# Zero products at the start, the second tile's output product by column halves, and identity products among the last rows

## The reference, cut to what matters

```python
h = rms_norm(x, norm2_g)                  # 256 x 1024
aff = softmax(h @ w_router)               # 256 x 16
# each of 16 experts takes its 32 best tokens, runs
# (silu(h @ w_gate) * (h @ w_up)) @ w_down, width 2816,
# and adds affinity * result to these tokens' rows of x
out = rms_norm(x, norm_f_g)
```

## Time and profile before

| | us |
|---|---|
| median of three runs | 2190.2 |
| lowest, highest run | 2189.45, 2190.91 |
| the profiled execution's own time | 2190.44 |
| its span | 2188.7 |
| PE busy (share of the span) | 1678.1 (77%) |
| DVE, ACT, POOL busy | 644.2, 310.7, 255.5 |

### The profile page before, as it was taken

One profiled execution on the slowest core, in us unless ns is written; L12 is line 12 of the kernel. 1 busy time (PEld: TensorE's weight loads), 2 busy tenths in 40 slices (PEclk: granted clock), 3 DMA queues, 4 the chain that ended last, 5 costly groups with the idle time before them and its releaser, 6 DMA issues.

```text
span 2188.7 us, 30640 instructions
## 1 busy us (share of the span) xinstructions
PE 1678.1 (77%) x13062; PEld 968.0 (44%) x13062; DVE 644.2 (29%) x1520; ACT 310.7 (14%) x739; POOL 255.5 (12%) x221
## 2 busy tenths in 40 slices
PE   8999999999999999995665565665656466466566
PEld 7867994886799476441221221221122122122122
DVE  3345777545477734320110010010010010010011
ACT  3231220324122013310000000000000000000001
POOL 0003880001388000000000000000000000000000
PEclk9999999999999999987777777777787777778778
DMA  8234652723554275489999999999999999999998
GB/s 316 79 116 145 215 181 96 255 79 116 164 173 175 96 263 235 200 374 430 433 433 434 431 427 434 435 435 434 433 426 433 435 435 434 434 431 427 435 434 345
DMA packets 99943, 695.12 MB, mean 318 GB/s; under 512 B 7627, under 2 KB 53067, under 8 KB 85773
## 3 DMA queue, kind: packets, MB, share of 16 engines
q1 hardware_dynamic: 96304, 684.71, 76.0%
q0 software_dynamic: 1712, 5.35, 0.7%
q10 hardware_dynamic: 1836, 3.80, 0.5%
HBM read 692.77 MB, written 4.22 MB: 318 GB/s over the span
## 4 chain that ended last, share of the span: by engine, by line
DMA 49%; PE 48%; DVE 1%; SPq 1%; ACT 1%; issue 0%; DVEq 0%; ACTq 0%
DMA arena<-in_gate_up 32%; DMA arena<-in_down_rows 17%; PE bank L1123 11%; PE bank L702 6%; PE bank L861 6%; PE bank L1348 6%; PE bank L676 3%; PE bank L1316 2%; PE bank L856 1%; PE bank L1182 1%; PE bank L1063 1%; PE bank L1186 1%; PE bank L1083 1%; PE bank L766 1%; PE bank L813 1%; PE bank L1209 1%
## 5 line engine op out<-in xcount | busy, mean ns | idle before, releaser
L1348 PE MATMUL bank<-arena 128*32 128x512 f32 (+1 forms) x3072 | 441.9, 741 | 366.0 <-DMA arena<-in_gate_up 365.5
L1348 PEld LDWEIGHTS bank<-arena 128*32 128x32 f32 x3072 | 112.5, 139 | 690.5 <-DMA arena<-in_gate_up 395.6
L2290 DVE TENSOR_TENSOR arena<-arena,bank 64x256 f32<-64x256 f32 x96 | 51.3, 535 | 766.3 <-ACT arena L1696 764.7
L1316 PE MATMUL bank<-arena 128*32 128x256 f32 x2816 | 204.5, 458 | 68.6 <-DMA arena<-in_down_rows 68.6
L1123 PE MATMUL bank<-arena 128*128 128x128 f32 x2128 | 238.0, 274 | 0.0
L1123 PEld LDWEIGHTS bank<-arena 128*128 128x128 f32 x2128 | 237.8, 192 | 0.0
L1316 PEld LDWEIGHTS bank<-arena 128*32 128x32 f32 x2816 | 101.0, 130 | 175.4 <-DMA arena<-in_down_rows 86.3
L861 PE MATMUL bank<-arena 128*128 128x256 f32 x576 | 138.6, 387 | 0.0
L1696 ACT ACTIVATE arena<-bank 64x512 f32<-64x512 f32 (+1 forms) x48 | 23.2, 550 | 809.0 <-PE bank L1348 809.0
L702 PE MATMUL bank<-arena 128*128 128x512 f32 x308 | 133.2, 592 | 0.0
L861 PEld LDWEIGHTS bank<-arena 128*128 128x128 f32 x576 | 104.7, 189 | 18.9 <-issue 4.6
(11 more groups left out here) (322 smaller groups left out, 1595.0 us busy)
## 6 DMA issues: line engine op xcount, KB each, us to landing
arena<-in_gate_up SPq DMA_DIRECT2D x60, 5632.0 KB, 46.2
arena<-in_down_rows SPq DMA_DIRECT2D x29, 5632.0 KB, 46.1
arena<-in_w_up SPq DMA_DIRECT2D x44, 1024.0 KB, 7.8
arena<-in_w_in SPq DMA_DIRECT2D x36, 1024.0 KB, 9.3
arena<-in_w_down SPq DMA_DIRECT2D x16, 1024.0 KB, 6.9
arena<-in_gate_up SPq DMA_DIRECT2D x5, 2816.0 KB, 12.3
arena<-in_w_out SPq DMA_DIRECT2D x12, 1024.0 KB, 6.1
arena<-in_w_down SPq DMA_DIRECT2D x12, 512.0 KB, 3.7
```

Of the source, the lines that this page charges most:

```text
L1316: done = mm(ps[5][32 * q:32 * q + 32, 0:256], hidden_t[:, r, 32 * half:32 * half + 32], weights[:, r - shift, 256 * q:256 * q + 256], star ...
L1348: last = mm(ps[b][32 * q:32 * q + 32, 0:n], expert_x[:, k, :], weights[:, c:c + n], start=(k == 0), stop=(k == KT - 1))
L2290: last = w.tensor_mul(hidden[64 * odd:64 * odd + 64, 2 * b:2 * b + m, :], blocks(expert_gate[0:64, c0:c0 + n]), blocks(ps[b][64:P, 0:n]))
```

## The change

Three stages are edited. At the start, DVE writes zeros into a piece of memory and TensorE makes six products of zeros by zeros into bank 7 before it waits for the first weights; ACT's constants and POOL's bias tables are issued only when `second_columns` has landed. At the router, tile 1's product goes by column halves, each half with a signal, an add and transposes of its own; both transposed halves of tile 1 are copied by DVE; the keep-clock product before the affinities' transposes has two blocks rather than four. At the end, three identity products stand between the first and the second of the last parts.

```diff
+START_PRODUCTS = (S, S, S, S, S, P)
...
+        zeros = normed_rows[:, 0, 0:S]
...
+            pool.wait_ge(sem("second_columns"), 16)
             pool.dma_start(bucket_table[0:BUCKETS + 1, :], a["bias_table"]).then_inc(sem("bias_in"), 16)
...
+                pe.wait_ge(sem("zeros_ready"), 1)
+                for n in START_PRODUCTS:
+                    mm(ps[7][:, 0:n], zeros[:, 0:P], zeros[:, 0:n], start=True, stop=True)
                 pe.wait_ge(sem("first_columns"), 16)
...
-            def rows_transposed(t):
-
-                pe.wait_ge(sem("second_rows"), t + 1)
-                for kh in range(2):
+            def rows_transposed(t, half=None):
+
+                for kh in range(2) if half is None else (half,):
+                    pe.wait_ge(sem("second_rows"), t + 1 + (kh if t else 0))
...
-                    pe.wait_ge(sem("h2_copied"), 2 * t + 2)
+                    pe.wait_ge(sem("h2_copied"), 2 * t + (1 if t else 2))
                 for k in ks:
+                    if t and k == KT // 2:
+                        pe.wait_ge(sem("h2_copied"), 4)
...
+            for nh in range(2):
                 for k in range(4):
...
+                    if nh == 0 and k == 2:
                         rows_transposed(0)
...
+                    last = second_product(1, k, nh)
+                if nh == 0:
+                    last.then_inc(sem("rows_t0"), 1)
+            last.then_inc(sem("rows_used"), 2)
+            rows_transposed(1, 0)
+            logits(0, range(2))
+            rows_transposed(1, 1)
+            logits(0, range(2, KT))
             logits(1, range(KT))
-            keep_clock(1)
+            keep_clock(1, 2)
...
+                            if i == 0:
+                                for _ in range(3):
+                                    keep_clock_on_rows(4)
...
+            act.wait_ge(sem("second_columns"), 16)
             act.dma_start(const[:, 0:2 * P + 4], a["consts"][:, 0:2 * P + 4]).then_inc(sem("ident_in"), 16)
...
+            w.memset(zeros, 0.0).then_inc(sem("zeros_ready"), 1)
...
                 for nh in range(2):
+                    if t:
+                        v.wait_ge(*((sem("rows_used"), (DEPTH + 1) * ROW_UNITS + 2) if nh else (sem("rows_t0"), at(L, "rows_t0", 2))))
                     xs = x[:, t, nh * 512:(nh + 1) * 512]
                     last = w.tensor_add(xs, xs, ps[ROWS_BANKS[2 * t + nh]][:, :])
-                last.then_inc(sem("second_rows"), 1)
-                v.wait_ge(sem("h2_transposed"), 2 * t + 2)
...
+                    if t or nh:
+                        last.then_inc(sem("second_rows"), 1)
+                for kh in range(2):
+                    if t or kh:
+                        v.wait_ge(sem("h2_transposed"), 2 * t + kh + 1)
...
```

More of the change, by code:

```diff
@@ L1253, in _, with second_product @@
             unit_in(L, 7)
-            for t in range(T):
+            def second_product(t, k, nh):
+                return mm(ps[ROWS_BANKS[2 * t + nh]][:, :], mixT[:, 4 + k, t * P:(t + 1) * P], slot(7, 1024)[:, k, nh * 512:(nh + 1) * 512], start=(k == 0), stop=(k == 3))
+            for k in range(4):
+                pe.wait_ge(sem("attended_read"), at(L, "attended_read", k + 1))
+                for nh in range(2):
+                    last = second_product(0, k, nh)
+            last.then_inc(sem("rows_t0"), 1)
+            for nh in range(2):
                 for k in range(4):
-                    if t == 0:
-                        pe.wait_ge(sem("attended_read"), at(L, "attended_read", k + 1))
-                    elif k == 1:
+                    if nh == 0 and k == 2:
                         rows_transposed(0)
[L1260 to L1265, removed]
+                    last = second_product(1, k, nh)
+                if nh == 0:
+                    last.then_inc(sem("rows_t0"), 1)
+            last.then_inc(sem("rows_used"), 2)
[3 more added lines that the diff above has]
+            logits(0, range(2, KT))
             logits(1, range(KT))
-            keep_clock(1)
+            keep_clock(1, 2)
             for t in range(T):
@@ L1306, in _, with keep_clock_on_rows @@
             gathered_transposed(1)
-            def keep_clock_on_rows():
-                mm(ps[1][:, :], ident, normed_rows[:, 0, 0:512], start=True, stop=True)
+            def keep_clock_on_rows(bank=1):
+                mm(ps[bank][:, :], ident, normed_rows[:, 0, 0:512], start=True, stop=True)
             def down_rows(half, weights, r0, n, shift=0):
@@ L1638, in rms @@
                 elif n == 1:
-                    act.wait_ge(sem("second_rows"), t + 1)
+                    act.wait_ge(sem("second_rows"), 2 * t + 1)
                 else:
@@ L1645, in rms @@
                     f(normed_rows[:, t, :], x[:, t, :], ACT.Square, accum_out=sum_sq[:, t:t + 1])
-                if n == 1:
-                    act.wait_ge(sem("h2_transposed"), 2 * t + 1)
+                if n == 1 and t == 0:
+                    act.wait_ge(sem("h2_transposed"), 1)
                     f(xT[:, 0:4, t * P:(t + 1) * P], ps[H2_BANKS[2 * t]][:, :].rearrange("p (x y) -> p x y", y=P), ACT.Copy).then_inc(sem("h2_copied"), 1)
@@ L2203, in second_rows @@
                     v.wait_ge(sem("rows_t0"), at(L, "rows_t0", 1))
-                else:
-                    v.wait_ge(sem("rows_used"), (DEPTH + 1) * ROW_UNITS + 2)
                 for nh in range(2):
+                    if t:
+                        v.wait_ge(*((sem("rows_used"), (DEPTH + 1) * ROW_UNITS + 2) if nh else (sem("rows_t0"), at(L, "rows_t0", 2))))
                     xs = x[:, t, nh * 512:(nh + 1) * 512]
                     last = w.tensor_add(xs, xs, ps[ROWS_BANKS[2 * t + nh]][:, :])
-                last.then_inc(sem("second_rows"), 1)
-                v.wait_ge(sem("h2_transposed"), 2 * t + 2)
-                w.tensor_copy(xT[:, 4:8, t * P:(t + 1) * P], ps[H2_BANKS[2 * t + 1]][:, :].rearrange("p (x y) -> p x y", y=P)).then_inc(sem("h2_copied"), 1)
+                    if t or nh:
[3 more added lines that the diff above has]
+                        v.wait_ge(sem("h2_transposed"), 2 * t + kh + 1)
+                        w.tensor_copy(xT[:, 4 * kh:4 * kh + 4, t * P:(t + 1) * P], ps[H2_BANKS[2 * t + kh]][:, :].rearrange("p (x y) -> p x y", y=P)).then_inc(sem("h2_copied"), 1)
                 if t == 1:
```

## The result

The changed kernel takes 2197.39 us (median of 14 runs, 2192.66 to 2203.38), against 2190.78 us (14 runs, 2189.14 to 2195.32) for the kernel before on the same chip: ratio 1.0031 with a 95% interval of 1.0024 to 1.0038. That is slower by more than the 0.2% named as the bound of "same". The forecast was 2188.8, its range ended at 2191.3, and "slower" had a chance of 0.02.

The account below looks back on a forecast made before the run. Half of the last-ending chain was DMA (experts wait for weights), nearly all the rest TensorE. Gains of 0 (start), 0.6 (router) and 0.8 us (end), 1.4 together, off the median 2190.2 gave 2188.8 us; range 2187.2 to 2191.3.

Parts of the forecast that it names:

- From there they run nearly without a gap to the end: a microsecond won here is one at the end.: Expert transfers, from the experts' start: they run nearly gapless, so 1 us won before them is 1 us at the end.
- the sum: Whole kernel: 0 at the start, 0.6 at the router and 0.8 at the end, 1.4 us gained.
- All of it still lands before that, so 27.13 stays.: Start: the moved transfers are small beside what precedes `conv_columns`, which still lands at 27.13 us.
- the start's 0: Start: TensorE's lead gains nothing at 34.26 us, since the key transposes wait for the chain from `conv_columns`; 0 us.
- First rival: Start: clock falls while TensorE waits 2.1 us before 34.26; costs 1.7 to 3.4 us, 2190.5 in all; chance 0.2.
- the rival's own worst: Start: clock stays low as long as at the router, costing 3.4 us; 2192.2 us in all.
- Start, TensorE's own steps.: Start: first 32 instructions begin at 5.8 to 6.0 and take 7.5 to 8 us; ACT still releases the key transposes.
- Router.: Router: selection starts 1.0 us earlier; expert 0 gains 0.6 us, out of 0.4 to 1.2 depending on the clock.
- the sign: Router: the first transposed choice comes only 0.4 to 0.8 us earlier if the forecast is right.
- End.: Last parts: identity products keep the clock up, the 56 instructions split at landings; gain 0.8 us, lower end 0.

Follow-up runs that it names:

- after_shifted: Changed kernel plus 58 tiny products in TensorE's waits ahead of the key transposes, 256 instructions added in all against the kernel before: 2191.43 us, ratio 1.0000.
- pad_16: Kernel before plus sixteen tiny zero products (64 instructions) at TensorE's start: 2203.23 us, ratio 1.0060.
- pad_2: Kernel before plus two tiny zero products (8 instructions) at TensorE's start: 2193.01 us, ratio 1.0006.
- moves_only: Kernel before with only ACT's constants and POOL's tables issued behind `second_columns`, no zero products: 2191.21 us, ratio 1.0003.
- pad_64: Kernel before plus 64 tiny zero products (256 instructions) at TensorE's start: 2192.93 us, ratio 1.0011.
- router_end: Kernel before with the router's and the end's edits, without the start's: 2189.03 us, ratio 0.9992.
- router_only: Kernel before with the router's edit alone: 2189.02 us, ratio 0.9993.
- start_warm: Kernel before with the start's edit plus eight identity products in TensorE's waits ahead of the key transposes, 56 instructions more: 2202.84 us, ratio 1.0055.

## Why the prediction was wrong, point by point

**"From there they run nearly without a gap to the end: a microsecond won here is one at the end."** Here the step failed that weighs most in the medians. Two terms of the sum were put at nothing and were not: the start (next point), and the experts' stretch, for which the sum has no term at all. The stretch measured +3.0 of the profiled 5.8 us, in an execution with one fetched pass, less than the start's 4.3. By the medians `after_shifted` gives back 5.9 of the 6.6 us; some 1.3 of that is a smaller loss by the clock (in its trace the transposes take 1.49 and the work behind them 8.34 us), which leaves some 4.6 for the loop. I costed the added instructions by their time at the place where they run. Their number moves everything behind them in TensorE's stream.

The loop's body is 1,687 instructions of TensorE: so many records lie from one of its closing branches to the next in the trace of the kernel before, in each of the six repeated passes (408 products of four, 16 transposes of two, and 23 others). That is 6.6 blocks of 256. It can lie in seven blocks, or across eight once its first instruction stands more than 105 behind a block's start. Results by shift: 0, +240 and +256 no repeated fetch; +8 and +24 some passes; +56 and +64 every pass; nine packets in each fetched pass, whatever the shift. An 8-block body from +56 on and a 7-block body at all others is what this count gives if the kernel before stands 50 to 81 behind a block's start; no run gives this position itself.

The Trainium skill, "Advanced Engine Details and Errata", ISA Cache, gives a cache line of 16 KB or 256 instructions and 128 KB for TensorE, thus eight blocks. The packets agree with the line's size. The same section of the Trainium skill says that there are only two cache lines; with that this case doesn't agree, since a body of 6.6 blocks ran six more times without a packet. By the 128 KB an 8-block body would just fit, but `pad_16` fetches nine blocks in each pass, more than the body has. That at least one block beyond the loop's end is fetched ahead of use, so that eight blocks and one more don't stay together, is my guess; it would also explain why a 7-block body that ends close to its last block's end (+8, +24) loses some passes and not others. Which passes, stays open: `pad_2` had two in its profiled run and the changed kernel one, and both kernels' runs scatter over 6 and 11 us.

**"All of it still lands before that, so 27.13 stays."** This is the other failed step, with which the start's 0 falls: the start measured +4.33 in the trace, 1.40 by this landing and 2.9 by the clock. `conv_columns` landed at 28.53. I counted the bytes of data in front of `conv_columns` and neither the 0.24 us of issue nor TensorE's instructions, whose packets share the DMA engines; that these are the cause is argued above and not shown. The moved issues, of which I was wary, cost 0.2 us in the median (`moves_only`).

**First rival, the clock falls in the wait.** Right as a mechanism, at the place and for the reason named, with a price of 1.7 to 3.4 us; it is 2.9 in the changed kernel's trace. The case against it, 0.22 of 1 us busy at a clock of 1.00, was a poor witness: that was one microsecond, here it is 3.8 us of waiting in 4.4. I gave it 0.2 since I took the wait as 2.1 us; the late landing made it longer. In `moves_only` the clock fell in the profiled execution too, behind 0.68 and 0.95 us of idle time, and in `pad_64` it stayed at 1.00 behind 0.72 and 0.95: with waits of this length it is a draw. The range ended at 2191.3, below the rival's own worst of 2192.2, and even that misses the result; only with the late landing and the loop does the sum come out.

**Start, TensorE's own steps.** Right: begin 5.78 (5.8 to 6.0), 32 instructions in 7.54 (7.5 to 8), transposes released by ACT, gain of 2.2 us that is worth nothing there.

**Router.** Right in its steps and too small in one. The rows of the router, on TensorE's and DVE's time lines, with all instants 4.33 us late by the start:

```profile
932.33 0.69 DVE L2229 TENSOR_TENSOR arena<-arena,bank 128x512 f32<-128x512 f32 x1 [0.90 <-PE bank L1263]
...
937.12 1.20 PE L1259 MATMUL bank<-arena 128*128 128x256 f32 x2
...
938.95 5.56 PE L1259 MATMUL bank<-arena 128*128 128x512 f32 x8
939.55 0.42 DVE L2266 MAX8 arena<-arena 16x8 f32<-16x256 f32 x1
```

The selection starts at 939.55 against 940.65, which is 936.32 moved by the 4.33: gain 1.10 (1.0 forecast). The first transposed choice comes at 944.44, 0.98 earlier than in the kernel before by the same reckoning, where 0.4 to 0.8 was named as the sign; the clock was low from 936.1 to 942.9 us. Expert 0 gains 0.97, where I took 0.6 out of 0.4 to 1.2. The medians give 1.6 and 1.7 us (`router_end`, `router_only`), and the stretch from tile 0's output product to expert 0 shows why: it took 31.3 to 33.4 us in the ten profiled kernels with the old router (32.43 in the kernel before, mean 32.7) and 30.6 to 31.5 in four with the new one (mean 31.0). Each execution draws its own, as the prediction allowed, and the one I read was a little better than the mean. By these the term is about 1.6, not 0.6, though both intervals of the medians still hold no gain at all.

**End.** The 56 instructions split at the landings as forecast, but the gain in the trace is 0.52 of the 0.8, and the medians show none: `router_end` and `router_only` differ by 0.01 us. `router_only` shows why, without the identity products, at its last parts:

```profile
2173.32 1.93 PE L1326 MATMUL bank<-arena 128*32 128x256 f32 x32 [2.38 <-DMA arena<-in_down_rows]
2175.77 1.07 PE L1326 MATMUL bank<-arena 128*32 128x256 f32 x16 [0.52 <-DMA arena<-in_down_rows]
2177.01 0.64 PE L1326 MATMUL bank<-arena 128*32 128x256 f32 x8 [0.17 <-DMA arena<-in_down_rows]
2178.29 1.90 PE L1414 MATMUL bank<-arena 32*128 32x256 f32 x16 [0.64 <-DVE arena L2308]
```

The clock is up although TensorE waited 2.38 us: 4.97 us from the second part to placing, as with the edit. The fallen clock of the earlier trace rows is one of two cases: of the eleven profiled executions without the edit five take 5.5 to 5.6 us from the second part to placing, and six take 5.0; the three with it take 4.98, 4.96 and 4.23. A row that hangs on the clock, read from one execution, is one draw of several.

The best version is the kernel before with the router's edit alone, 2189.02 us: by the two comparisons 8.3 us faster than the changed kernel and 1.7 faster than the one before, though that interval, 0.9984 to 1.0002, still holds 1.

## What to carry to other kernels

Before instructions are added ahead of a hardware loop, count its body in blocks of 256 instructions, as they stand in the trace (here four for a product and two for a transpose), and keep it well clear of an eighth block; read the instruction queue's packets before and after, since a loop that no longer fits was fetched in every pass here and the page's chain calls it waiting for weights. Where a loss appears in a stretch that nobody edited, pad the stream by a whole block: if the loss goes, it was the position. And filling work that wins time in front of a wait for DMA wins nothing, but lengthens that wait, which can cost the clock.

## What the runs showed of the hardware

- A loop of 1,687 TensorE instructions in seven iterations stays without a fetch in its six repeated passes (`before`). Its stretch takes 10.5 to 10.7 us more when its start moves by 64 or 56 instructions (`pad_16`, `start_warm`), and 0.1 more when it moves by 256 (`pad_64`). Nine packets are fetched in each such pass.
- A fetched pass costs 1.8 to 3.2 us (1.8 where every pass is fetched). The bytes don't explain it: nine packets are 0.15 MB, 0.34 us at the 433 GB/s of that stretch. TensorE waiting for its first instructions would explain some (7.2 to 8.6 us of waiting at the head of a single fetched pass, against 6.7 at most where nothing is fetched); a packet of some 1.0 us on one DMA engine may also hold up one sixteenth of a transfer that all 16 share. How much each does was not separated.
- Waits of 2.82 and 0.94 us with 0.64 us of narrow products between them brought TensorE's clock to its lower level for 6.8 us. Eight identity products of 256 columns in the same waits kept it up (`start_warm`). Waits of 0.68 and 0.95 us brought it down for 3.4 us in one execution (`moves_only`), waits of 0.72 and 0.95 did not in another (`pad_64`).
